# Attention: maxima products placed in twos, with both banks' waits ahead of the first

## The reference

```
# layer 0, per block of queries: three softmaxes, each with its own keys and values
s_c = einsum('bqghd,bngd->bghqn', qb, k_cmp)      # 63 compressed blocks ("cmp")
s_s = einsum('bqghd,bgqkd->bghqk', qb, k_s)       # selected blocks ("full")
s_w = einsum('bqghd,bkgd->bghqk', qb, k_w)        # window of 512 ("near")
p   = masked_softmax(s, mask)                     # in float32
o   = gb[..., 0:1] * o_c + gb[..., 1:2] * o_s + gb[..., 2:3] * o_w
# layer 1: indexer scores choose 256 keys per query, then one softmax over them
_, sel = lax.top_k(score, top_k)
s = einsum('bqhd,bqkd->bhqk', qb, k_s);  p = masked_softmax(s, sel <= t)
```

## Time and profile before

| | us |
|---|---|
| median of 3 runs | 3317.99 |
| lowest, highest | 3314.23, 3318.42 |
| the profiled execution | 3313.27 |
| its span | 3311.4 |

### The profile page before, as it was taken

The page is one execution under the profiler, slowest core; times in us unless marked ns, Lnnn a source line. Parts: engine busy times, 40 slices in busy tenths (PEclk is TensorE's granted clock), DMA queues, the critical chain, the costliest instruction groups (busy, mean ns, idle before and its releaser), DMA issues.

```text
span 3311.4 us, 35561 instructions
## 1 busy us (share of the span) xinstructions
PE 2954.5 (89%) x12424; PEld 2233.1 (67%) x12424; DVE 2072.8 (63%) x3708; ACT 1511.4 (46%) x2593; POOL 277.7 (8%) x221
## 2 busy tenths in 40 slices
PE   7797999999879999999968685479997999999997
PEld 5685556665667888878856564245566788887885
DVE  6544455554267776677675699754426777667656
ACT  4343555555344544444433554445434454444443
POOL 2352000000000000000003034130000000000000
PEclk9887999999989999999989798689998999999999
DMA  5133121111323333333313012442142233333332
GB/s 169 44 99 108 46 53 40 52 47 40 125 66 94 96 96 96 96 96 93 98 58 111 1 53 81 102 141 52 33 126 66 89 96 98 93 96 96 105 102 73
DMA packets 356617, 275.05 MB, mean 83 GB/s; under 512 B 58085, under 2 KB 308007, under 8 KB 355927
## 3 DMA queue, kind: packets, MB, share of 16 engines
q1 hardware_dynamic: 355287, 270.68, 27.6%
q10 hardware_dynamic: 1152, 2.10, 0.2%
HBM read 238.18 MB, written 31.92 MB: 82 GB/s over the span
## 4 chain that ended last, share of the span: by engine, by line
PE 76%; DVE 12%; ACT 4%; issue 3%; DMA 3%; SPq 1%; POOL 0%; POOLq 0%; DVEq 0%; ACTq 0%
PE PS L491 18%; PE PS L492 18%; PE PS L493 18%; PE PS L909 10%; PE PS L830 3%; PE PS L884 3%; PE PS L885 3%; DVE m_MASK L2290 2%; PE PS L890 1%; DVE m_Z L2364 1%; DVE m_PRED L2295 1%; DVE RT_b L596 1%; DMA WR<-in_nsa_w_out 1%; PE PS L645 1%; PE PS L902 1%
## 5 line engine op out<-in xcount | busy, mean ns | idle before, releaser
L491 PE MATMUL PS<-HH,WH 128*128 128x512 f32 (+1 forms) x2160 | 857.4, 397 | 91.8 <-POOL WL L464 47.6
L492 PE MATMUL PS<-HL,WH 128*128 128x512 f32 (+1 forms) x2160 | 849.3, 393 | 0.0
L493 PE MATMUL PS<-HH,WL 128*128 128x512 f32 (+1 forms) x2160 | 847.9, 393 | 0.0
L491 PEld LDWEIGHTS PS<-HH,WH 128*128 128x128 f32 x2160 | 414.3, 192 | 186.4 <-issue 56.5
L492 PEld LDWEIGHTS PS<-HL,WH 128*128 128x128 f32 x2160 | 413.7, 192 | 86.6 <-issue 2.5
L493 PEld LDWEIGHTS PS<-HH,WL 128*128 128x128 f32 x2160 | 413.2, 191 | 86.2
L480 DVE TENSOR_TENSOR WL<-WR,WH 128x1024 fp32r<-128x1024 f32 x290 | 354.2, 1221 | 111.4 <-ACT WH L473 99.4
L473 ACT ACTIVATE WH<-WR 128x1024 fp32r<-128x1024 f32 x290 | 308.1, 1062 | 123.8 <-PE PS L493 90.2
L929 ACT ACTIVATE n_PX<-PS 128x512 f32<-128x512 f32 (+1 forms) x320 | 173.0, 544 | 223.3 <-PE PS L890 114.2
L1028 DVE CUSTOM_DVE_ANT_0 n_JUNK<-PS,n_MZ 128x512 bf16<-128x512 f32 (+2 forms) x320 | 147.9, 488 | 116.8 <-PE PS L830 116.5
L460 POOL TENSOR_TENSOR TOUCH<-WR 128x1 f32<-128x1 f32 x45 | 10.1, 225 | 1867.5 <-PE PS L493 1029.5
(11 more groups left out here) (375 smaller groups left out, 5166.9 us busy)
## 6 DMA issues: line engine op xcount, KB each, us to landing
WR<-in_ffn_w_up SPq DMA_DIRECT2D x176, 512.0 KB, 3.7
WR<-in_ffn_w_down SPq DMA_DIRECT2D x88, 512.0 KB, 3.4
WH<-qh_save SPq DMA_DIRECT2D x64, 256.0 KB
n_RB<-r_save SPq DMA_DIRECT2D x96, 128.0 KB, 2.9
WR<-in_nsa_w_out SPq DMA_DIRECT2D x16, 512.0 KB, 3.8
WL<-ql_save SPq DMA_DIRECT2D x32, 256.0 KB
WR<-in_dsa_w_in SPq DMA_DIRECT2D x16, 512.0 KB, 4.0
WR<-in_dsa_w_out SPq DMA_DIRECT2D x16, 512.0 KB, 4.0
```

Source lines behind the costliest of these rows:

```text
L491: nc.tensor.matmul(dst, wh, xh, start=start, stop=False)
L492: nc.tensor.matmul(dst, wh, xl, start=False, stop=False)
L493: return nc.tensor.matmul(dst, wl, xh, start=False, stop=stop)
```

## The change

Two things. The plan counts the peaks placed behind round 0; one with an even count goes by its time as before, one with an odd count goes to the step of the peak before it. And in `ring_pe` two peaks that stand next to each other in a step are taken as a pair: the waits for both banks stand ahead of the first product, and the second has none of its own. Which maximum is computed from what, and the order of the peaks, stay the same.

```diff
@@ place_peaks
+        pairs = 0
         for x, p in enumerate(self.peaks):
             if p.r == 0:
                 step = -1
             else:
                 us = when[x] if p.r < 3 else max(when[x], self.begin[self.ends[p.r - 3] + 1] + 5.0)
-                step = max(self.step(us), seen)
+                step = max(self.step(us), seen) if pairs % 2 == 0 else seen
+                pairs += 1
@@ ring_pe
-            for y in a.plan.ring_at.get(step, ()):
+            def bank_free(y):
                 if y >= 3:
                     what, x = a.plan.ring[y - 3]
                     if what == "peak":
                         pe.wait_ge(a_md, a.md0 + x + 1)
                     else:
                         pe.wait_ge(a_me, a.me0 + x + 1)
+
+            ys = list(a.plan.ring_at.get(step, ()))
+            while ys:
+                y = ys.pop(0)
                 what, x = a.plan.ring[y]
...
+                both = bool(ys) and a.plan.ring[ys[0]][0] == "peak"
+                if both:
+                    bank_free(ys[0])
+                peak_pe(pe, a, y, x)
+                if both:
+                    y = ys.pop(0)
+                    peak_pe(pe, a, y, a.plan.ring[y][1])
```

More of the change, by code:

```diff
@@ L842, in ring_pe @@
                         pe.wait_ge(a_me, a.me0 + x + 1)
+            ys = list(a.plan.ring_at.get(step, ()))
+            while ys:
+                y = ys.pop(0)
                 what, x = a.plan.ring[y]
-                if what == "peak":
-                    peak_pe(pe, a, y, x)
-                else:
+                bank_free(y)
+                if what == "rows":
                     pe.wait_ge(a_md, a.md0 + a.plan.total[x])
@@ L850, in ring_pe @@
                                         IDENT[:, :]).then_inc(a_pk, 1)
+                    continue
+                both = bool(ys) and a.plan.ring[ys[0]][0] == "peak"
[5 more added lines that the diff above has]
+                    peak_pe(pe, a, y, a.plan.ring[y][1])
         def scores_pe(pe, a, u):
```

## The result

The changed kernel takes 3352.75 us (median of 4 runs, 3348.75 to 3357.14). The kernel before, run beside it, takes 3318.2 (4 runs, 3314.23 to 3318.57). The ratio is 1.0107, with a 95% interval from 1.009 to 1.0125: 34.6 us slower, where 27.2 were forecast (3345, range 3328 to 3357). The profiled execution of after took 3351.79, with a span of 3350.0, so the spans differ by 38.6.

What follows compares the result with a forecast made beforehand. The prediction took TensorE as the bound, with no slack in the second attention's late part. Its six terms summed to 27.2 us on the profiled 3313.27, giving 3345 us after adding the 4.7 difference to the median; range 3328 to 3357.

Steps and rivals of the forecast that it cites:

- Bound: Second attention's late part: PE busy 157.66 of 158 us, so each added us of waiting is a us of time.
- term 1: Second attention, rounds 9 to 15: steps of three become four, second pair waits a round trip; 11.3 us (0 to 15).
- Term 2: First attention, step 0: 26 products become 13 pairs, each waiting a round trip at low clock; 7.2 us (3.5 to 9).
- Term 3: First attention, step -1: 18 products of mixed widths, wider ones issued later; 1.5 us (0 to 3).
- term 4: Second attention, steps -1 and 0: 16 products of mixed widths at the low clock; 1.4 us (0 to 3).
- Term 5: Second attention, rounds 2 to 8: new and old steps of four, round 8's twelve in one step; 3.5 us (0 to 6).
- dearer: Rival: in rounds 2 to 8 waits keep the clock at its lower level, 10 us more, 3355; chance 0.10.
- Term 6: First attention, steady part: in seven steps of four the third product waits too; 2.3 us (-2 to 4).
- The mask: Second attention, step 10: the transpose's 4.89 us wait goes, but ScalarE is held by the same mask; priced at 0.
- a rival at 4.9: Rival: the removed wait at the mask pays in full, 4.9 us less, 3340; chance 0.14.
- Met waits: Second products of pairs lose 274 waits; a wait already met costs nothing, so removing them gains 0.
- the signs named: Late second attention: some 14 waits of 0.8 us, PE busy 158 of about 170; first values product about 8.5 us later.

Runs made afterwards that it cites:

- cold steps plain: Changed kernel, but in steps -1 and 0 of both attentions each maxima product waits for its own bank alone; 3342.69 against 3314.37 us for the kernel before.
- waits alone: Kernel before with its places kept, but within a step both banks' waits stand ahead of a pair's first product; 3333.21 against 3313.33 us, ratio 1.0064.
- one pair a step: Changed kernel, but a step's second pair goes to the next step, except in rounds 0, 1 and second attention's round 8; 3335.33 against 3313.33 us before.
- only the cold steps: Kernel before, with a pair's two waits ahead of its first product only in the first attention's steps -1 and 0; 3326.43 against 3314.46 us.
- a mere delay: Two kernels: the kernel before, with VectorE writing its table 60 or 50 times more ahead of the first attention; 3331.38 against 3314.78, 3331.67 against 3314.46 us.

## Why the prediction was right, and where it was not

- **Bound, and term 1.** The late rounds had no slack: 14 steps of four cost 13.9 to 14.1 us, and 28 cost 27.7, none of it hidden. The size was 0.81 a time and measured 0.99. Two pieces were missing. From a maximum's end to the product's start are 0.15 us (2296.98 to 2297.13) and not 0.07. And the second pair starts on an idle PE: its products stand 0.31 apart (2297.13 and 2297.44), where a 512-wide product is otherwise followed after 0.23. Together that is 0.16 of the 0.18.
- **Term 2** (7.2) measured 7.1, by the mechanism forecast. At the low clock pairs are 1.65 apart instead of 1.59; some of the pairs ran at the upper clock, which took it back. **Term 3** (1.5) measured 2.2 and **term 4** (1.4) 1.4.
- **Term 5 failed.** The prediction said of rounds 2 to 8 that the new fours cost 0.4 and the old ones 0.17, counted half of that, and had 3.5 in all (0 to 6). The changed kernel lost 15.9 there. The missing mechanism was among the rivals, "dearer", at 10 us and a chance of 0.10: the clock falls to its lower level in steps 1 to 11, which has some 5 of the 7.3 lost in them. I had taken each stretch's clock from the trace of before as given, and term 4's 1.4 us as harmless. Alone, term 4's waits cost 9.9 by the median; in the trace 1.8 of it is theirs and 4.4 stand in the steps behind. Much of the rest is size: round 8's twelve and four in steps 39 to 41 cost 5.0, where 2.0 was worked out; the clock is low there from 2239.5 to 2256.6 (a mean of 0.60 over the three steps, 0.68 before), and the pairs are again 1.65 apart. Steps 12 to 38 have 3.8, of which 2.2 can come without any change there. Alone, these rounds cost 8.8, and with the cold steps plain steps 1 to 48 still cost 8.9: the term was too small by its own waits too, not only by the clock that the cold steps let fall.
- **Term 6** (2.3) measured 3.1 with steps 1 to 6. PE's waits for maxima rose by 5.9 us (from 5.7 to 11.6) and the stage by less, since ScalarE's eviction covers the fours.
- **The mask.** Priced at 0, against a rival at 4.9: the wait went (-5.7 in step 12), came back as ScalarE's, and the kernel with this move alone has a ratio of 0.9997. Right.
- **Met waits** at 0: the late rounds of the kernel with waits alone cost +0.4, though each pair there waits in another place. Nothing was gained by the 274 waits removed. Right.
- **The total** lay in the range in part by luck. The attentions cost 43.7 us in the profiled execution, 16.5 more than the sum of the terms; 7.4 came back between them, outside the change, which nothing in the prediction foresaw; the measured medians differ by 34.6. The range itself does not follow from the terms: their own bounds add up to 1.5 and 40 us, 3320 to 3358, and not to 3333 to 3355. Of the signs named, the waits (14 of 1.06) and PE's busy 161 of 172 came; the first values product starts 10.4 us later than before and not 8.5, 1.2 of it from ahead of the attention.

Whose the 7.4 us are stays open. What they consist of is shown for 5.3 of them; another 2.1 are there by 990 us, and no run explains them. Behind 1930 us DVE searches thresholds with small operations (128x6), while GpSimd works on queries and weights. Before, DVE and then POOL:

```profile
1990.18 1.21 DVE L2296 TENSOR_TENSOR m_STEP<-m_PRED,m_PW 128x6 f32<-128x6 f32 x1
1991.43 0.17 DVE L2300 TENSOR_TENSOR m_CAND<-m_CM,m_STEP 128x6 f32<-128x6 f32 x1
...
1994.57 1.81 DVE L2292 TENSOR_TENSOR m_CM<-m_CAND,m_PW 128x6 f32<-128x6 f32 x1
...
1990.08 1.29 POOL L2012 TENSOR_TENSOR m_ROT<-m_ROT,m_SIN 128x512 f32<-128x512 f32 x1
...
1994.02 2.34 POOL L464 TENSOR_TENSOR WL<-WR,WH 128x1024 fp32r<-128x1024 f32 x1
```

The same operation takes 0.17 us or, when a GpSimd operation is under way, until that one ends: 1990.18 + 1.21 = 1991.39, and POOL's (1990.08 + 1.29) ends at 1991.37; 1994.57 + 1.81 = 1996.38 against 1994.02 + 2.34 = 1996.36. Of the 124 such operations 31 are long in the kernel before, every one ending within 0.06 us of a GpSimd operation, and they lose 35.5 us together. An operation that starts just ahead of GpSimd's is not held (0.16 at 1988.80, GpSimd's at 1988.83), nor are the three that lie inside a GpSimd memset, which reads nothing (2070.04 to 2072.69; 0.17 each). In the changed kernel 28 are long and lose 30.2. One group of them, before and after:

```profile
L2295 DVE TENSOR_TENSOR m_PRED<-m_CNT,m_KT 128x6 f32<-128x6 f32 x31 | 19.3, 622 | 1.1
```

```profile
L2308 DVE TENSOR_TENSOR m_PRED<-m_CNT,m_KT 128x6 f32<-128x6 f32 x31 | 17.2, 556 | 1.1
```

What decides how many collide is not shown. Three kernels gained (-7.4, -7.1 and -4.8: the changed one, one pair a step, waits alone), all with the waits ahead throughout the first attention and its cold steps, and in them these operations lose 30.2, 29.8 and 30.2. In each of the other eleven traces exactly 31 are long, and they lose 35.5 to 35.7. The kernels with only the cold steps (-0.2), with all but the cold steps (+1.1), and with a mere delay (+1.9, +1.7) did not. In the changed kernel the first sign in that stretch is a DMA's result that GpSimd waits 8.26 us for instead of 7.17, at 2001.44; in the kernel with the waits alone the gain comes only behind 2052. Each kernel has one profiled execution, but eleven that agree to 0.2 us and three that agree to 0.4 speak against mere chance of an execution.

No version tried beats the kernel before; the best, one product moved ahead of the mask, can't be told from it.

## What to carry to other kernels

Two waits ahead of a pair are free where other work stands between two pairs, and cost a whole round trip (here 0.99 us of a busy engine, 0.67 of it by the place alone) where a second pair stands right behind: count the places that hold more products than banks, not the waits. Where the clock has just risen, price a lengthened step by what runs behind it too: 1.8 us in the cold steps brought 4.4 more in the steps behind, in the trace, and 9.9 in all by the median. And before a wait is credited as a gain, ask what else its releaser holds up: the 4.9 us ahead of the transpose behind the mask were worth nothing that could be measured.

## What the runs showed of the hardware

- A DVE operation on two SBUF inputs of 6 columns takes 0.17 us, or lasts until the GpSimd operation that was running when it started ends: 31 of 124, 35.5 us in this kernel, in a stretch in which VectorE is busy 163 of 168 us (1930 to 2098). It is not held where it started first, nor beside a GpSimd memset. The Trainium skill states the mechanism ("SBUF — State Buffer", Who interferes with whom): the two engines share a port pair as an exclusive lock, and a DVE instruction with two SBUF inputs contends with a GpSimd instruction that reads SBUF. By that rule the searches' accumulating reductions, with one input, should not be held; the trace agrees (the 128x768 one lasts 1.01 us in the 10 cases beside GpSimd's work and in the 21 without it).
- The same step 0, 6.09 and 6.10 us long, left the clock up in one execution and let it fall within the next step in another. Step 1 then lasted 2.37 instead of 1.35 us, with the same instructions.
- From the end of a maximum to the start of a product that waited for it are 0.15 us, and the product's own maximum starts 0.52 us after it at 2.4 GHz (2295.77 to 2296.29) and 0.80 at 1.2 GHz (332.76 to 333.56).
